# Running the second layer's and the hybrid layer's weight products inside their attention steps, in a three-layer transformer kernel on one core

## What is computed

```python
for i in (0, 1):                       # first block
    a = mixer_i(rms_norm(h, g))        # i = 0: MLA, i = 1: differential attention
    h = h + rms_norm(a, g)
    h = h + rms_norm(conv_ffn(rms_norm(h, g)), g)

def diff_mixer(x, w_qkv, ...):         # 8 heads, two maps of width 64, values of 128
    q, k, v = split(x @ w_qkv)
    p = softmax(q k^T * scale - slope * dist)        # for both maps
    a = (p[:, :, 0] - lam * p[:, :, 1])              # lam: one learned number
    o = rms_norm(a @ v, subln_g) * (1 - lam_init)    # norm over each head's 128
    return o @ w_o

def hybrid_layer(x, ...):              # the third layer
    qa, ka, va, qb, kb, vb, qi, ki, wi, ga, gb = split(rms_norm(x) @ w_in)
    o_a = causal attention(qa, ka, va)               # 8 heads of 64, with RoPE
    o_b = attention(qb, kb, vb) on the 64 keys of each query that the index
          score of qi, ki, wi ranks highest          # 8 heads of 64
    x = x + (sigmoid(ga) * (o_a @ w_proj_a) + sigmoid(gb) * (o_b @ w_proj_b)) @ w_out
    return x + hier_moe(rms_norm(x))                 # 32 experts, 2 per token
```

## Time and profile before

| | us |
|---|---|
| median of 3 runs | 1425.67 |
| lowest, highest | 1424.09, 1430.08 |
| the profiled execution | 1426.64 |
| its span, from first to last instruction | 1424.8 |
| mean granted clock of TensorE in it | 0.978 of full |
| TensorE, VectorE, ScalarE, GpSimd busy | 1331.2, 557.5, 545.0, 570.0 |

### The profile page before, as it was taken

How to read it: one execution, slowest core, us unless ns; L and a number is a source line. 1 busy time by engine, 2 the same in 40 slices (tenths; PEclk the granted TensorE clock), 3 DMA queues, 4 the chain that set the end, 5 groups by cost and what they waited for, 6 DMA issues and landing times.

```text
span 1424.8 us, 19820 instructions
## 1 busy us (share of the span) xinstructions
PE 1331.2 (93%) x7721; PEld 970.8 (68%) x7721; DVE 557.5 (39%) x1199; ACT 545.0 (38%) x850; POOL 570.0 (40%) x132
## 2 busy tenths in 40 slices
PE   6999999999977899999999897889999999999996
PEld 5767999998856799998888574674454454444442
DVE  4543444443264444445456487241121111112112
ACT  4553655555455455555454645211111111111112
POOL 5532888885642398787568552300000000000000
PEclk9999999999998999999999998989999999999999
DMA  7631665654531286664345421568999999999995
GB/s 265 211 89 59 198 187 187 197 200 156 177 118 30 71 245 188 188 196 155 132 165 179 146 89 59 222 250 341 423 422 423 422 423 422 423 423 423 423 423 229
DMA packets 164259, 341.20 MB, mean 239 GB/s; under 512 B 11001, under 2 KB 113754, under 8 KB 139610
## 3 DMA queue, kind: packets, MB, share of 16 engines
q1 hardware_dynamic: 164186, 340.18, 64.5%
HBM read 339.10 MB, written 1.05 MB: 239 GB/s over the span
## 4 chain that ended last, share of the span: by engine, by line
PE 78%; DVE 9%; DMA 7%; ACT 2%; SPq 2%; issue 1%; POOL 1%; ACTq 0%; DVEq 0%
PE bank L590 16%; PE bank L592 16%; PE bank L591 16%; PE bank L1054 12%; DMA ring<-in_w 6%; PE bank L1078 6%; PE bank L1005 4%; PE bank L689 2%; SPq L525 2%; PE bank L600 1%; PE bank L1035 1%; PE bank L721 1%; DVE att L1613 1%; DVE room L1609 1%; DVE xn L1637 1%
## 5 line engine op out<-in xcount | busy, mean ns | idle before, releaser
L552 POOL TENSOR_TENSOR low<-raw,high 128x2048 fp32r<-128x2048 f32 (+4 forms) x128 | 569.8, 4479 | 349.0 <-ACT high L1123 349.0
L590 PE MATMUL bank<-xh,high 128*128 128x256 f32 x872 | 243.6, 279 | 6.4 <-POOL low L552 4.1
L1123 ACT ACTIVATE high<-raw 128x2048 fp32r<-128x2048 f32 (+4 forms) x128 | 234.8, 1847 | 26.5 <-PE bank L590 18.4
L591 PE MATMUL bank<-xl,high 128*128 128x256 f32 x872 | 242.7, 278 | 0.0
L592 PE MATMUL bank<-xh,low 128*128 128x256 f32 x872 | 242.6, 278 | 0.0
L1054 PE MATMUL bank<-ring,room 128*64 128x512 f32 x768 | 228.3, 595 | 6.4 <-DMA ring<-in_w 4.8
L590 PEld LDWEIGHTS bank<-xh,high 128*128 128x128 f32 x872 | 163.8, 188 | 9.4 <-POOL low L552 4.5
L592 PEld LDWEIGHTS bank<-xh,low 128*128 128x128 f32 x872 | 165.1, 189 | 0.0
L591 PEld LDWEIGHTS bank<-xl,high 128*128 128x128 f32 x872 | 163.8, 188 | 0.7
L590 PE MATMUL bank<-high,xh 128*128 128x512 f32 (+4 forms) x400 | 153.9, 385 | 10.4 <-DVE xl L1502 4.8
L592 PE MATMUL bank<-high,xl 128*128 128x512 f32 (+4 forms) x400 | 151.3, 378 | 0.0
(11 more groups left out here) (208 smaller groups left out, 1821.2 us busy)
## 6 DMA issues: line engine op xcount, KB each, us to landing
ring<-in_w SPq DMA_DIRECT2D x144, 1024.0 KB, 24.3
raw<-in_ffn_w_up SPq DMA_DIRECT2D x88, 512.0 KB, 4.9
room<-in_w SPq DMA_DIRECT2D x24, 1024.0 KB, 21.1
xspare<-in_w SPq DMA_DIRECT2D x24, 1024.0 KB, 26.0
raw<-in_ffn_w_down SPq DMA_DIRECT2D x44, 512.0 KB, 3.9
raw<-in_w_in SPq DMA_DIRECT2D x44, 512.0 KB, 4.2
raw<-in_diff_w_qkv SPq DMA_DIRECT2D x24, 512.0 KB, 4.6
raw<-in_mla_w_o SPq DMA_DIRECT2D x8, 512.0 KB, 5.1
```

What stands on the lines that cost most here:

```text
L552: pool.tensor_tensor(low[:, p % PARTS, 0:n], raw[:, p % RING, 0:n], high[:, p % PARTS, 0:n], ALU.subtract).then_inc(low_ready, 1)
L590: first = pe.matmul(out_, a[0], b[0], start=start, stop=False)
L591: pe.matmul(out_, a[0], b[1], start=False, stop=False)
L1123: act.activation(high[:, p % PARTS, 0:n], raw[:, p % RING, 0:n], ACT.Copy).then_inc(high_ready, 1)
```

## The change

Only the order, the banks and the place of some VectorE and ScalarE work change; what is computed does not.

**Second layer.** The pieces of `diff_w_qkv` are reordered (q0 k0 q1 k1 q2, then v0 k2 v1 q3 v2 k3 v3; each value piece is now half the rows of 512 columns). Five of them come before the attention. Steps 0 to 6 hold one piece each, steps 8 and 10 one of `diff_w_o`, and two follow. The attention uses banks 0 and 1 for scores, 2 for transposes, 3 for outputs of two heads together; products use banks 4 to 7. Outputs are no longer copied by ScalarE: it takes their squares from the bank for each pair of heads (now with `squares` and a semaphore `pair_squares`) and guesses the scale factors of the pair; VectorE refines them and scales the pair out of the bank (`outputs_scaled`, steps 5, 7, 9, 11). The transposes of a pair follow one step later. For two maps ScalarE's copy of the transposes and what is beside now come before the exponentials.

**Hybrid layer.** The two attentions become one of 16 heads (`hyb_att`). The products with vb, the gates a and b and the projections, and the transposes of kb, lie in its steps, one piece each in steps 0 to 9 and in 10, 12 and 16; one follows. VectorE does one of the 8 top-8 rounds in each of steps 0 to 7, and the product of gate a with its projection in step 13.

```diff
-STAGES = {"mla_att": (MH, 1), "diff_att": (DH, 2), "moba_att": (8, 1), "dsa_att": (8, 1)}
+STAGES = {"mla_att": (MH, 1), "diff_att": (DH, 2), "hyb_att": (16, 1)}
+QKV = ["q0", "k0", "q1", "k1", "q2", "v0", "k2", "v1", "q3", "v2", "k3", "v3"]
...
     (plan)
+    def diff_beside(s):
+        if s in (6, 8, 10):
+            groups(f"diff_t{s // 2 - 3}", 1, [2])
+        if s in (0, 4):
+            groups(f"diff_v{s // 4}", 2, [4, 5])
+        elif s in (1, 3, 5):
+            groups(f"diff_q{s}", 1, [6])
+        elif s == 8:
+            groups("diff_o", 4, [4, 5, 6, 7])
+    attention("diff_att", diff_beside, ([0, 1], 2, 3), paired=True)
...
+    attention("hyb_att", hyb_beside, ([0, 1], 2, 3))
...
     (TensorE)
+            for n in range(5):
+                two_heads(G["diff_q"] + n, W["qkv"] + n)
+            def diff_beside(s):
+                if s in (6, 8, 10):
+                    outputs_transposed(s // 2 - 3)
+                if s in (0, 2, 4, 6):
+                    by_token(G[f"diff_v{s // 4}"], W["qkv"] + 5 + s, X, [4], [512], k_from=2 * (s % 4), k_all=KT)
+                elif s in (1, 3, 5):
+                    two_heads(G[f"diff_q{s}"], W["qkv"] + 5 + s)
+                elif s in (8, 10):
+                    moved(pe, G[f"diff_t{s // 2 - 4}"])
+                    square_out("diff_o", W["diff_wo"], X, s // 2 - 4, 1)
+                if s in (3, 7):
+                    for t in range(NT):
+                        moved(pe, G[f"diff_v{s // 4}"] + t)
...
-            outputs_moved("diff_att")
-            keep_clock(4, begin(G["diff_t"]))
...
-            square_out("diff_o", W["diff_wo"], X)
+            moved(pe, G["diff_t2"])
+            square_out("diff_o", W["diff_wo"], X, 2, 1)
+            outputs_transposed(3)
+            moved(pe, G["diff_t3"])
+            square_out("diff_o", W["diff_wo"], X, 3, 1)
...
+            def hyb_beside(s):
+                if s < 2:
+                    by_token(G["vb"], W["vb"] + s, X, [4], [512], k_from=4 * s, k_all=KT)
+                    if s == 0:
+                        rotated("kb")
+                elif s < 10:
+                    name = ("ga0", "ga1", "gb0", "gb1")[s // 2 - 1]
+                    by_token(G[name], W["vb"] + s, X, [4], [512], k_from=4 * (s % 2), k_all=KT)
+                elif s in (10, 12):
+                    projected("a", s // 2 - 5)
+                elif s == 16:
+                    projected("b", 0)
...
     (ScalarE, attention)
+                    if maps == 2:
+                        between(s)
+                        if 2 <= s < heads + 2:
+                            g = tr[s - 2]
+                            copy(g, pT[:, s % 2].rearrange("p k q -> p (k q)"), bank[BANK[g]][:, :])
...
     (ScalarE, outputs of the second layer)
+                if hd % 2:
+                    full(act, g)
+                    for x in range(4):
+                        at = 2 * (hd - 1) + x
+                        squares(ss_o[:, at:at + 1], b[:, P * x:P * x + P], score[:, x // 2, P * (x % 2):P * (x % 2) + P],
+                                pair_squares)
+                    act.wait_ge(pair_squares, 2 * (hd + 1))
+                    guess(rs_o[:, 2 * hd - 2:2 * hd + 2], ss_o[:, 2 * hd - 2:2 * hd + 2], P)
...
     (ScalarE, hybrid)
+                split(min(W["vb"] + s + 3, W["pa"] + max(s // 2 - 2, 0) if s < 14 else W["pb"] + 3))
...
     (VectorE)
+            def outputs_scaled(m):
+                dve.wait_ge(pair_squares, 4 * m + 4)
+                r = rs_o[:, 4 * m:4 * m + 4]
+                refined(r, ss_o[:, 4 * m:4 * m + 4], P, 4)
+                g = A_["diff_att"][2][2 * m]
+                full(dve, g)
+                dve.tensor_tensor(otok[:, :, S * m:S * m + S].rearrange("p t (j d) -> p j t d", d=P),
+                                  bank[BANK[g]][:, :].rearrange("p (j t d) -> p j t d", j=2, t=NT),
+                                  spread(r3(r, b=NT), 2, NT, P), ALU.mult).then_inc(bank_moved[BANK[g]], 1)
+                moved(dve, g)
+                dve.tensor_copy(st[:, 27:28], r[:, 0:1]).then_inc(o_ready, 1)
+            def diff_beside(s):
+                if s in (5, 7, 9, 11):
+                    outputs_scaled((s - 5) // 2)
+                elif s in (6, 8, 10):
+                    outputs_low(s // 2 - 3)
...
+            def hyb_beside(s):
+                if s < TOPK // 8:
+                    for t in range(NT):
+                        ins = dve.max(top8[:, t, :], work[s % 2][:, t, :])
+                    link(ins)
+                    for t in range(NT):
+                        ins = dve.match_replace(work[1 - s % 2][:, t, :], top8[:, t, :], work[s % 2][:, t, :], -3e38)
+                    link(ins)
...
+                if s == 13:
...
+                            dve.tensor_tensor(x, bank[BANK[g]][:, :], x, ALU.mult).then_inc(bank_moved[BANK[g]], 1)
```

More of the change, by code:

```diff
@@ L474, in _ @@
             ffn(0, behind0)
-            weights(W["qk"], A["diff_w_qkv"][0], [(0, 8, 256 * n, 256) for n in range(8)])
-            pre_gains(3, A["norm_g"][1, 2])
-            post_gains(2, A["norm_g"][1, 1])
-            for n in range(2):
-                weights(W["v"] + 2 * n, A["diff_w_qkv"][0][:, 2048 + 512 * n:2560 + 512 * n], two)
+            for x, name in enumerate(QKV):
+                n = int(name[1])
+                if name[0] == "v":
+                    piece = (4 * (n % 2), 4, 2048 + 512 * (n // 2), 512)
+                else:
+                    piece = (0, 8, 1024 * (name[0] == "k") + 256 * n, 256)
+                weights(W["qkv"] + x, A["diff_w_qkv"][0], [piece])
+                if x == 4:
+                    pre_gains(3, A["norm_g"][1, 2])
+                    post_gains(2, A["norm_g"][1, 1])
             square(W["diff_wo"], A["diff_w_o"][0])
@@ L953, in projected @@
-            def projected(name, a, x):
-                outputs_moved(name)
-                square_out("p" + a, W["p" + a], x)
-            def branch(name, a, q_, k_, v_, beside):
-                attention(name, halves(q_), halves(k_), lambda hd, k: v_[:, k, 64 * hd:64 * hd + 64], False,
-                          lambda s: [] if s else [G[x] + t for x in ("q" + a + "_t", "k" + a + "_t", "v" + a)
-                                                  for t in range(NT)], beside)
-            branch("moba_att", "a", qaT, kaT, va, lambda s: gates("a") if s == 1 else None)
@@ L1216, in attention @@
                                     ins.then_inc(bank_moved[BANK[sc[s, 0]]], 1)
-                    if between:
+                    if between and maps == 1:
                         between(s)
-                    if s == heads and name != "moba_att":
+                    if s == heads and name in ("mla_att", "hyb_att"):
                         load_table(ACT.Abs_reciprocal_sqrt)
-                    if 2 <= s < heads + 2:
+                    if maps == 1 and 2 <= s < heads + 2:
                         g = tr[s - 2]
@@ new lines, in _, with outputs_high @@
+            for x in range(5):
+                split(W["qkv"] + x + 3)
+                two_heads(G["diff_q"] + x, QKV[x])
+            def outputs_high(m):
+                g = G[f"diff_t{m}"]
+                high_part(g, xh[:, 2 * m:2 * m + 2, :].rearrange("p a b -> p (a b)"), bank[BANK[g]][:, :], st[:, 15:16])
+            def diff_beside(s):
+                if s in (6, 8, 10):
+                    outputs_high(s // 2 - 3)
+                split(min(W["qkv"] + s + 8, W["diff_wo"] + (s + 2) // 2 - 2 if s > 6 else W["ffn1"]))
+                if s in (1, 3, 5):
+                    two_heads(G[f"diff_q{s}"], QKV[5 + s])
+                elif s in (2, 6):
@@ L1349, in diff_values @@
                     for t in range(NT):
[L1350 to L1352 removed]
+                        g = G[f"diff_v{s // 4}"] + t
+                        copy(g, vtok[:, t, 512 * (s // 4):512 * (s // 4) + 512], bank[BANK[g]][:, :])
             def head_out(g, hd, b):
[L1356 to L1359 removed]
@@ L1826, in _ @@
-            link(dve.tensor_scalar(selm, work[0], -2e38, -NEG, ALU.is_le, ALU.mult))
-            link(dve.scalar_tensor_tensor(selm, selm, NEG, caus, ALU.add, ALU.add))
-            def gate_a():
-                for g in range(G["ga"], G["ga"] + 4):
-                    moved(dve, g)
-                for t in range(NT):
-                    for hf in range(2):
-                        g = G["pa"] + 2 * t + hf
-                        full(dve, g)
-                        x = siga[:, t, 512 * hf:512 * hf + 512]
-                        dve.tensor_tensor(x, bank[BANK[g]][:, :], x, ALU.mult).then_inc(bank_moved[BANK[g]], 1)
@@ L1842, in _ @@
+            dve.wait_ge(roped, rotations[roped.name])
+            attention("hyb_att", HD_SCALE, lambda s: (selm if s >= 8 else caus, 1.0), output, beside=hyb_beside)
+            for n in range(2):
+                for t in range(NT):
+                    moved(dve, G[f"gb{n}"] + t)
             for t in range(NT):
```

192 lines of the change are left out of this document (91 added, 101 removed).

## The result

The changed kernel takes 1432.78 us (median of 12 runs, 1430.46 to 1441.48), the kernel before 1426.62 (12 runs, 1424.09 to 1430.82). The ratio is 1.0044, 95% interval 1.0030 to 1.0057: 6.2 us slower. The profiled execution took 1432.28 us with a span of 1430.5, 5.7 more than the span of before.

What follows compares the result with a forecast made beforehand. TensorE's chain through both attention stretches to the experts' start was taken as the bound. Second layer -4.3 and hybrid layer +5.5 gave +1.2 us on the profiled 1426.64, so 1427.8, or 1426.9 for the median; range 1412 to 1445.

Steps and rivals of the forecast that it cites:

- The bound: Both attention stretches: a microsecond won or lost in either moves the end by one; nothing in the expert stage changes.
- the GpSimd term: Second layer, steps 0 to 6: seven GpSimd low parts hold up VectorE operations; 0 to 11 us, taken as 6.
- step 5, without holds: Second layer: wait for VectorE's scaling of a pair in the shared bank, 6.4 us mostly covered by a product: 0.3 us.
- step 7: Second layer: wait for the scaled pair in the shared bank, with no product as cover: 5.8 us.
- step 9: Second layer: wait for squares, table load, guess, refinement and scaling of a pair, less the transposes: 4.2 us.
- slow clock: Second layer: half-speed heads behind three gaps of TensorE, 1.5 us each: 4.5 us.
- The steps 0 to 9: Hybrid layer: a loop of mean 8.2 us against TensorE's 8.3 per step; cost 0 to 8 us, taken as 4.
- The bank: Hybrid layer: one bank for outputs makes TensorE wait in steps 11, 13, 14 and 15: 5.6 us.
- The clock: Hybrid layer: slow clock behind two gaps of about 4 us: 3.0 us.
- The first: Both layers: low parts fall where VectorE idles or reads banks, dense products hold the clock up; 1410 us, chance 0.26.
- The second: Both layers: low parts hold VectorE nearly their whole length, so VectorE sets the step; 1444 us, chance 0.33.
- The third: Both stretches stay because the products still queue behind old waits; 1425.7 us, chance 0.03.

Runs made afterwards that it cites:

- short low parts: Changed kernel with GpSimd making only 128 of 2048 columns of low parts in both attentions: 1410.70 us; the same cut in the kernel before: 1416.31 us.
- gated low parts: Changed kernel with GpSimd's low parts in the attention steps waiting until VectorE has finished the step's probabilities (step 5: scaled the pair): 1413.41 us.
- experiment 5: Changed kernel with TensorE making products that nobody reads in its gaps of the second layer: 1426.29 us, ratio 1.0000 to before.
- the halves: Each half of the change alone, the other half's lines as before: second layer's half 1.0002 of before, hybrid half 1.0046.
- four pair banks: Changed kernel with the second layer's four pairs of outputs in banks 3, 7, 3 and 0 instead of all in bank 3: 1426.76 us.
- three edits together: Changed kernel with gated low parts, four pair banks and two outputs of the hybrid layer in flight: 1402.45 us.
- second layer's half alone: Kernel before with only the second layer's half of the change, hybrid layer as before: 1428.51 us, ratio 1.0002.

## Why the prediction came out as it did

The prediction said 1426.9 us, range 1412 to 1445, within 0.5% of before the likeliest at 0.41; it was 1432.78, 0.44% slower. The case and the range held, and the point was 5.9 us too low. That it was not further off is partly luck: the errors of the stretches add to 7.9 us, and some 3 us came back in between for a reason that the prediction didn't have.

**The bound.** Right. The experts' first load moved by 5.68 us and the span by 5.7; nothing was won or lost behind it.

**Second layer: the step that failed is the size of the GpSimd term.** Predicted 22.3 us left over, a stretch of 134; measured 141.2 - 112.1 = 29.1.

| left over in the second layer | predicted | measured | from |
|---|---|---|---|
| step 5, without holds | 0.3 | 0.6, 0.3 | short and gated low parts |
| step 7 | 5.8 | 5.8 | the wait |
| step 9 | 4.2 | 3.7 | the wait |
| last transposes | 1.5 | 1.6 | the wait |
| holds by GpSimd | 6 (0 to 11) | 11.2 | 8.0 - 0.6 + 3.8 |
| slow clock | 4.5 | 5.3 | experiment 5 |
| not accounted for | 0 | 0.9 | 29.1 less the rows above |

The waits for the one bank were right to half a microsecond, built from rows of single operations. Rows 8 had shown a hold of 3.33 us; what I didn't see is where it bites. In steps 0 to 4 five holds of 2.1 to 4.9 us cost TensorE nothing at once, as its step of 8.3 us covers them. In steps 5 and 6 two holds count in full: 7.4 us in step 5, of which its own hold is 4.3 and the delay left by step 4's is 3.1, and 3.8 us in step 6. I had written that there they lie directly on the path, and then priced all seven with one middle value. The term should have been priced by place: the first four at nothing, the fifth at what it leaves to step 5, the last two at their whole length.

**Hybrid layer: right in sum, by errors of opposite sign.** In the bounds of the prediction (from the first work of the attention) it became 147.9 us where 147 was said; left over 25.4 for 24.5. The steps 0 to 9: 2.6 us of waits for 4. The bank: 10.75 us of waits in steps 11 to 15. Of these, holds are 3.7 (2.40 and 1.65 less 0.17 each) where 6 was predicted, the gate products about 1.0 for 1.4, and the bank itself 6.0 for 5.6. The last three outputs 2.6 for 3.0, the start 1.5 for 1.5. The clock is the term that was mis-sized: 147.9 less 122.5 of work and 17.7 of waits leaves 7.7 us, for 3.0 predicted. I had counted two gaps at 1.5 us, the price of one head behind a gap. There were three, and behind two of them a weight piece followed, which ran slow as well, at least in part: the first, from 863.59 to 870.49, took 6.9 us where a piece is 5.6. No run fills the gaps of this layer, so the 7.7 us are a remainder and not a measurement of the clock.

**The sum.** +1.2 was predicted, 6.2 measured on the medians. Taken by stretches I was wrong by 6.6 us in the second layer (+2.3 for -4.3) and by 1.3 in the hybrid one (+6.8 for +5.5), together 7.9, and the profiled execution of the changed kernel gave some 3 us net back in between. By the ratios of the halves (+0.3 and +6.6) the errors are 4.6 and 1.1 us: the second layer's is the larger one either way.

**The rivals.** The first (low parts fall where VectorE idles) is what gating makes true: 1410 was its time, 1413.4 the gated kernel's. The second (VectorE sets the step) came in part: the five holds of steps 0 to 4 lasted 3.8 us in the mean and so passed its threshold of 3.4, and VectorE had no idle time from 360.42 to 411.5 us, one of the signs named for this rival. But steps with a piece stay at about 8.2 us, because VectorE began them well ahead of need (26.2 us idle before 360.42), and its lag reached TensorE only in step 5, as 3.1 of the 7.4 us there. The rest of the loss came through the steps without cover. The third is refuted by the waits of the earlier trace rows, which are gone.

**What I had not asked** is what the kernel before paid to the same cause. I counted its 19.0 us of removable time in the hybrid layer as fill and drain of an attention. Cutting its low parts took 13.2 us off that stretch (9.6 us of the whole time by the ratio), so most of it was two held operations and the slow clock behind them, which two waits in GpSimd's program remove without any new order. The 5.5 us of loss in the hybrid half were right as a number, but the alternative to compare with was not the old stretch of 142 us but one of about 129.

## What to carry to other kernels

When work moves beside an attention, look up in the trace which small operations of VectorE last as long as GpSimd's, and price each by whether TensorE has a product to do at that point: under cover it costs nothing, without cover its whole length and a slow head or piece behind it. Then try the cheap cures first: let GpSimd wait for a mark in VectorE's program, and write operations on a few columns one column at a time. A gap that a new bank closes tends to open again one instruction later, so read what is queued next before counting it as won.

## What the runs showed of the hardware that I had not expected

**Two paces of the same products.** A turn of the feed-forward loop takes 16.40 or 16.82 us, at a granted clock of 1.00 in both, and each of the two blocks keeps one of these values in all but single turns. Of 28 blocks in 14 profiles, 23 ran at 16.40; at 16.82 ran the second block of before, of the short low parts, of the four pair banks and of the three edits together, and the first block of the gated low parts. Over a block that is 4 us, two thirds of what the change costs. It goes with no order of the kernels: with the order of before, the second block is slow in the profile of before and fast in that with short low parts. Whether it varies between executions of one kernel is not shown, as each kernel has one profile, and what sets it is open. Products of 512 columns don't show it (0.229 us apart in all).

**One execution's clock.** The same hybrid code lost 8 us more in one profile than in another with nearly equal waits (14.2 and 14.9 us). The granted clock was 0.87 instead of 0.93 over the stretch, and between 800 and 820 us 0.60 instead of 0.83. First the profile with the larger loss (second layer's half alone), then before:

```profile
800.00:820.00 20.00, 15.13 (x43) 8.15 (x42) 13.73 (x26) 10.03 (x24) 4.71 (x2) 0.60 0.31 105
```

```profile
800.00:820.00 20.00, 14.85 (x60) 8.27 (x59) 17.11 (x35) 11.35 (x31) 4.50 (x1) 0.83 0.30 106
```

A difference of a few microseconds between two profiles is therefore no proof about a change; the waits repeat to within a microsecond, the slow stretches don't.
